# One wide query projection in place of two narrow ones, ahead of an expert layer's row gathers

## The reference

```
def peer(xn, wq, subkeys, u, v):              # xn: 256 x 2048
    q = (xt @ wq).reshape(T, 8, 2, 128)       # wq: 2048 x 2048, 8 heads, 2 sides
    s1 = einsum('thd,nd->thn', q[:, :, 0], subkeys[0])      # 128 keys on each side
    s2 = einsum('thd,nd->thn', q[:, :, 1], subkeys[1])
    v1, i1 = top_k(s1, 16);  v2, i2 = top_k(s2, 16)
    sc, ci = top_k(all 16 x 16 sums of v1 and v2, 16)
    idx = i1[ci // 16] * 128 + i2[ci % 16]    # 128 experts of each token
    gate = softmax(sc)
    h = gelu(xc . u[ic])                      # u: 16384 x 2048, rows gathered by idx
    return sum over the 128 of gate * h * v[ic]             # v: 16384 x 2048
```

## Time and profile before

| | |
|---|---|
| median of 3 runs | 3982.63 us |
| lowest and highest run | 3982.62 and 3986.85 us |
| profiled execution: span from first to last instruction | 3985.6 us |
| profiled execution: own time | not listed apart; its span is 3.0 us over the median and 1.25 us under the highest run |
| TensorE busy | 2187.0 us, 55% of the span |
| VectorE busy | 1962.2 us, 49% |
| GpSimd busy | 1297.3 us, 33% |
| ScalarE busy | 343.6 us, 9% |
| moved by DMA | 932.83 MB, 637.57 MB of it on the queue of GpSimd's gathers and loads |

### The profile page before, as it was taken

The page is one execution under the profiler, slowest core; times in us unless marked ns, Lnnn a source line. Parts: engine busy times, 40 slices in busy tenths (PEclk is TensorE's granted clock), DMA queues, the critical chain, the costliest instruction groups (busy, mean ns, idle before and its releaser), DMA issues.

```text
span 3985.6 us, 26773 instructions
## 1 busy us (share of the span) xinstructions
PE 2187.0 (55%) x8774; PEld 1503.0 (38%) x8774; DVE 1962.2 (49%) x2297; ACT 343.6 (9%) x713; POOL 1297.3 (33%) x712
## 2 busy tenths in 40 slices
PE   0899853588999999998898898700000000000000
PEld 0444642545888887443448756700000000000000
DVE  7664165311000000001004511799998888888887
ACT  0000222101011110000103501000000000000000
POOL 2111140000000000000000000177788888888886
PEclk9999875789999999999997999955555555555555
DMA  9898200023444444443640035799899999999998
GB/s 375 333 416 349 67 34 0 1 86 136 157 148 152 153 148 147 157 148 115 203 144 18 0 110 187 282 403 411 341 416 391 374 390 372 374 373 376 378 359 340
DMA packets 236362, 932.83 MB, mean 234 GB/s; under 512 B 20059, under 2 KB 25363, under 8 KB 164115
## 3 DMA queue, kind: packets, MB, share of 16 engines
q0 software_dynamic: 99840, 637.57, 40.1%
q1 hardware_dynamic: 136197, 294.46, 21.7%
q10 hardware_dynamic: 272, 0.13, 0.0%
HBM read 928.91 MB, written 2.15 MB: 234 GB/s over the span
## 4 chain that ended last, share of the span: by engine, by line
PE 50%; DVE 22%; DMA 10%; POOL 8%; issue 6%; ACT 2%; DVEq 0%; SPq 0%; POOLq 0%; ACTq 0%
PE ps L789 16%; PE ps L1041 15%; PE ps L1054 8%; DVE x L1811 6%; POOL ring L456 4%; DVE ring L1773 4%; DVE proj L1773 4%; PE ps L1189 3%; POOL proj L456 3%; DMA ring<-in_w_in 3%; DMA proj<-in_peer_v,proj 2%; DMA ring<-in_peer_u,proj 2%; DMA ring<-in_peer_v,proj 2%; DMA arena<-in_w_mod 1%; DVE arena L1261 1%
## 5 line engine op out<-in xcount | busy, mean ns | idle before, releaser
L447 POOL COPY proj<-proj 128x8 int32 x64 | 109.8, 1716 | 1999.7 <-DVE proj L1746 1957.0
L1041 PE MATMUL ps<-hT,ring 128*128 128x256 f32 x2816 | 608.0, 379 | 1.4 <-ACT hT L488 1.4
L1041 PEld LDWEIGHTS ps<-hT,ring 128*128 128x128 f32 x2816 | 535.0, 190 | 74.3 <-issue 1.7
L789 PE MATMUL ps<-ring,hT 128*128 128x512 f32 (+2 forms) x1216 | 492.8, 567 | 12.1 <-DMA ring<-in_w_in 10.7
L1811 DVE SCALAR_TENSOR_TENSOR x<-proj,x 128x2048 f32<-128x2048 f32 x128 | 301.3, 2354 | 84.2 <-DMA proj<-in_peer_v,proj 73.7
L789 PEld LDWEIGHTS ps<-ring,hT 128*128 128x128 f32 x1216 | 226.1, 197 | 279.0 <-issue 255.4
L1811 DVE SCALAR_TENSOR_TENSOR x<-ring,proj,x 128x2048 f32<-128x2048 f32 x128 | 301.0, 2352 | 30.2 <-DMA ring<-in_peer_v,proj 13.4
L1054 PE MATMUL ps<-ring,arena 128*128 128x512 f32 x704 | 304.1, 595 | 2.7 <-ACT arena L651 2.7
L456 POOL DMA_INDIRECT ring<-in_peer_v,proj x128 | 291.9, 2281 | 39.0 <-issue 39.0
L1773 DVE CUSTOM_DVE_ANT_0 proj<-proj,yT 128x2048 f32<-128x2048 f32 x128 | 288.5, 2289 | 21.4 <-DMA proj<-in_peer_u,proj 18.2
L1773 DVE CUSTOM_DVE_ANT_0 ring<-ring,yT 128x2048 f32<-128x2048 f32 x128 | 289.5, 2292 | 18.6 <-DMA ring<-in_peer_u,proj 17.5
(11 more groups left out here) (379 smaller groups left out, 2250.8 us busy)
## 6 DMA issues: line engine op xcount, KB each, us to landing
arena<-in_w_mod POOLq DMA_DIRECT2D x96, 1024.0 KB
ring<-in_w_in SPq DMA_DIRECT2D x68, 1024.0 KB, 12.8
ring<-in_ffn_w_gate SPq DMA_DIRECT2D x44, 1024.0 KB, 5.1
ring<-in_ffn_w_up SPq DMA_DIRECT2D x44, 1024.0 KB, 5.2
ring<-in_ffn_w_down SPq DMA_DIRECT2D x44, 1024.0 KB, 4.8
ring<-in_w_out SPq DMA_DIRECT2D x32, 1024.0 KB, 5.1
ring<-in_peer_wq SPq DMA_DIRECT2D x32, 1024.0 KB, 5.0
arena<-bias_rows SPq DMA_DIRECT2D x1, 4096.0 KB, 14.4
```

The costliest lines, as they stand in the source:

```text
L447: pool_eng.tensor_copy(expert_now[:, half, :], expert[:, t, bass.ds(i * (2 * ROWS) + ROWS * half, ROWS)]).then_inc(sem("experts_now"), 1)
L789: ins = pe.matmul(ps[:, 2 * (b % 2) + t, 0:w], lhs[:, KS * s + k, P * t:P * (t + 1)], ring[:, s, k, 0:w], start=(s == 0 and k == 0), stop= ...
L1041: ins = pe.matmul(ps[:, 4 * m + f, 0:T], ring[:, s, k, P * f:P * (f + 1)], hT[:, KS * s + k, :], start=(s == 0 and k == 0), stop=(s == SLO ...
```

## The change

TensorE now runs the query projection once, with both token tiles as 256 moving columns: four blocks in place of eight, in banks 0 to 3 and 4 to 7 in turn. The weights are streamed once. ScalarE copies 4 x 256 columns for each block. The second block waits for `keys_out`, since the turned keys lie in bank 4. After the fourth block's copy come tile 0's scores into banks 0 to 3 and at once tile 1's into banks 4 to 7, and ScalarE copies eight banks out. VectorE's and GpSimd's programs stay as they were, but for the block count in GpSimd's wait and one small memset that is dropped.

```diff
-for _n, _c in (... ("out2", 4), ("wq", 8)):
+for _n, _c in (... ("out2", 4), ("wq", 4)):
...
-        for t in range(NT):
-            stream(w1v["peer_wq_2"], BLK["wq"] + 4 * t, 4, 0)
+        stream(w1v["peer_wq_2"], BLK["wq"], 4, 0)
...
-                                pool_eng.wait_ge(*at("unit_used", SLOTS * (BLK["wq"] + 4 * NT)))
+                                pool_eng.wait_ge(*at("unit_used", SLOTS * (BLK["wq"] + 4)))
...
+        with act.Fori(0, 2) as i:
+            for par in range(2):
+                act.wait_ge(*at("unit_used", i * (2 * SLOTS) + SLOTS * (BLK["wq"] + par + 1)))
+                act.copy(peer["q"][:, bass.ds(i * 8 + 4 * par, 4), :], ps[:, 4 * par:4 * par + 4, 0:T]).then_inc(sem("wq_out"), 1)
         for t in range(NT):
-            with act.Fori(0, 4) as i:
-                act.wait_ge(*at("unit_used", i * SLOTS + SLOTS * (BLK["wq"] + 4 * t + 1)))
-                act.copy(peer["q"][:, bass.ds(i * 4, 4), P * t:P * (t + 1)], ps[:, 0:4, 0:P]).then_inc(sem("wq_out"), 1)
             for b in range(4):
                 act.wait_ge(*at("keys_scored", t * 4 + b + 1))
-                act.copy(peer["score"][:, t, 4 * b:4 * b + 4, :], ps[:, 4 + b, :]...).then_inc(sem("score_out"), 1)
+                act.copy(peer["score"][:, t, 4 * b:4 * b + 4, :], ps[:, 4 * t + b, :]...).then_inc(sem("score_out"), 1)
...
+        def wq_block(i, par):
+            for s in range(SLOTS):
+                pe.wait_ge(sem(f"slot{s}"), i * 32 + 16 * (BLK["wq"] + par + 1))
+                for k in range(KS):
+                    for f in range(4):
+                        ins = pe.matmul(ps[:, 4 * par + f, 0:T], ring[:, s, k, P * f:P * (f + 1)], hT[:, KS * s + k, :],
+                                        start=(s == 0 and k == 0), stop=(s == SLOTS - 1 and k == KS - 1))
+                ins.then_inc(sem("unit_used"), 1)
+
+        wq_block(0, 0)
+        pe.wait_ge(*at("keys_out", 1))
+        wq_block(0, 1)
+        for par in range(2):
+            pe.wait_ge(*at("wq_out", par + 1))
+            wq_block(1, par)
+        pe.wait_ge(*at("wq_out", 4))
         for t in range(NT):
-            with pe.Fori(0, 4) as i:
-                ...
-            pe.wait_ge(*at("wq_out", 4 * t + 5))
-            if t == 0:
-                pe.wait_ge(*at("keys_out", 1))
-            else:
-                pe.wait_ge(*at("score_out", 4))
             for c in range(SIDES):
-                ins = pe.matmul(ps[:, 4 + c // 4, P * (c % 4):P * (c % 4 + 1)], ...)
+                ins = pe.matmul(ps[:, 4 * t + c // 4, P * (c % 4):P * (c % 4 + 1)], ...)
...
-        link(vec.memset(stat[:, 24:25], 0.0), "wq_out")
```

More of the change, by code:

```diff
@@ L54 @@
 _b = 0
-for _n, _c in (("in1", 12), ("out1", 4), ("up", 22), ("down", 11), ("in2", 7), ("out2", 4), ("wq", 8)):
+for _n, _c in (("in1", 12), ("out1", 4), ("up", 22), ("down", 11), ("in2", 7), ("out2", 4), ("wq", 4)):
     BLK[_n] = _b
@@ L723, in _ @@
         norm_cols(3, vc("ffn_norm2", 0, 16), None)
+        with act.Fori(0, 2) as i:
+            for par in range(2):
+                act.wait_ge(*at("unit_used", i * (2 * SLOTS) + SLOTS * (BLK["wq"] + par + 1)))
+                act.copy(peer["q"][:, bass.ds(i * 8 + 4 * par, 4), :], ps[:, 4 * par:4 * par + 4, 0:T]).then_inc(sem("wq_out"), 1)
         for t in range(NT):
-            with act.Fori(0, 4) as i:
-                act.wait_ge(*at("unit_used", i * SLOTS + SLOTS * (BLK["wq"] + 4 * t + 1)))
-                act.copy(peer["q"][:, bass.ds(i * 4, 4), P * t:P * (t + 1)], ps[:, 0:4, 0:P]).then_inc(sem("wq_out"), 1)
             for b in range(4):
                 act.wait_ge(*at("keys_scored", t * 4 + b + 1))
-                act.copy(peer["score"][:, t, 4 * b:4 * b + 4, :], ps[:, 4 + b, :].rearrange("p (a b) -> p a b", b=P)).then_inc(sem("score_out"), 1)
+                act.copy(peer["score"][:, t, 4 * b:4 * b + 4, :], ps[:, 4 * t + b, :].rearrange("p (a b) -> p a b", b=P)).then_inc(sem("score_out"), 1)
         for t in range(NT):
@@ L1180, in _ @@
         ins.then_inc(sem("keys_turned"), 1)
-        for t in range(NT):
-            with pe.Fori(0, 4) as i:
[L1184 to L1191, removed]
-            pe.wait_ge(*at("wq_out", 4 * t + 5))
-            if t == 0:
-                pe.wait_ge(*at("keys_out", 1))
-            else:
-                pe.wait_ge(*at("score_out", 4))
+        def wq_block(i, par):
[13 more added lines that the diff above has]
+        pe.wait_ge(*at("wq_out", 4))
+        for t in range(NT):
             for c in range(SIDES):
-                ins = pe.matmul(ps[:, 4 + c // 4, P * (c % 4):P * (c % 4 + 1)], peer["q"][:, c, P * t:P * (t + 1)], peer["keysT"][:, c % 2, :],
+                ins = pe.matmul(ps[:, 4 * t + c // 4, P * (c % 4):P * (c % 4 + 1)], peer["q"][:, c, P * t:P * (t + 1)], peer["keysT"][:, c % 2, :],
                                 start=True, stop=True)
```

## The result

The changed kernel takes 4031.43 us (median of 4 runs, 4029.68 to 4038.03) against 3983.47 us (4 runs, 3982.62 to 3986.85): ratio 1.0121, interval 1.0107 to 1.0136, or +48.0 us. The forecast was 4029 us in a range of 4020 to 4038, +46.8 us.

What follows compares the result with a forecast made beforehand. The start of the second stage, through tile 0's scores and choice, bounds the kernel; a delay is carried to the end. Terms +50.3 - 7.9 + 4.4 = +46.8 us, giving 4029 us on the median, range 4020 to 4038.

Steps and rivals of the forecast that it cites:

- The hinge: Query projection between the two stages: it matters by when the second stage can begin, not by how busy TensorE is.
- Projection, +50.3 us: Joint pass of 512 instructions with 256 columns takes 110.5 us, so tile 0's scores start 50.3 us later.
- Rival B: Projection pass: weight loading sets the pitch at 0.192 us, pass 98.3 us, 12 us less, 4017 us; chance 2%.
- Weights, `keys_out`, the memset, straight code: 0 each: Around the projection: saved weight traffic, the wait for turned keys, the dropped memset and unlooped TensorE code each change nothing.
- Choice, 52.7 us: VectorE's choice of tile 0's experts: same instructions, still 52.7 us, experts at 2608.4.
- ScalarE's wait, -7.9 us: Before tile 0's dot products: the 13.96 us wait falls to 2.6; they begin 7.75 us after the experts, not 15.7.
- Arrival of the slots, +4.4 us: First sixteen dot products: gathered slots arrive at DMA's pace, not already waiting, losing 3.6 to 5.4 us.
- -3.5: Lead left at the first dot products after slower slot arrival: 2.5 to 4.3 us, taken as 3.5.
- "The shift stays.": After the first dot products: group pitch 41.07 us is VectorE's, DMA needs 39.4 to 41.2, so the delay persists.
- Rival C: Gather stages from 2922 us on settle into another beat, 10 us either way: 4019 or 4040; chance 5%.
- the prediction's chances: Whole kernel: slower 98%, 1% faster 1%, the same 1%; the forecast itself 91%.

Runs made afterwards that it cites:

- wait_both: The kernel before, with VectorE beginning tile 0's choice only when both tiles' scores are out (score_out 8 in place of 4); ratio 1.0145.
- pick_later: The kernel before, with tile 0's pick_weights and its wait for ScalarE's exponential moved behind the first sixteen dot products; ratio 0.9998.
- wide_early: The changed kernel, with both tiles' four sides of each block scored and chosen while the next block runs; ratio 1.0091 to the kernel before.
- the three early kernels: Choice cut by blocks: on the kernel before 1.0048, the same with each slot's gather freed by own last use 1.0035, on the changed kernel 1.0091.

## Why the prediction was right, step by step

**The hinge.** The prediction read that the choice for tile 0, not TensorE's second pass, feeds the next stage, although the chain named the pass. wait_both shows it: a start of the choice 65 us later, and nothing else, costs 58 us.

**Projection, +50.3 us.** Measured +50.5 (the pass 110.7 us, predicted 110.5; the copy 1.01). The price from the row of the same shape held to 0.2 us. Rival B falls by the same row. By the spacings of the Trainium skill, "TensorE: Matmul & The Clock Gate", section "Back-to-back issue gap", the pass would have taken an estimated 94 us; this trace disagrees, 0.216 us an instruction.

**Weights, `keys_out`, the memset, straight code: 0 each.** TensorE has no gap between its 512 matmuls, with idle time 0.0 in its group.

**Choice, 52.7 us.** Measured 52.7.

**ScalarE's wait, -7.9 us.** Measured -8.4: the first dot product 7.3 us after the experts, predicted 7.75. The term was right in size and in what is late next (the first slot), usable 5.6 us after its gather was issued where the prediction added up 6.06. The exponential was cheaper than the 2.6 us taken: its table load ran 48.77 us ahead of its activation, in ScalarE's idle time.

**Arrival of the slots, +4.4 us.** The first group is 5.0 us longer, the whole stage 3.6 and 6.0. With the term before it this makes -4.8 and -2.4 in place of -3.5. pick_later, which has these two terms almost alone, ends at 0.9998, so their sum cannot be told from nothing.

**"The shift stays."** Right, but one reason was wrong in part. The prediction took the first stage's pitch as VectorE's because VectorE was 99% busy. wide_early shows that the rate of the gathers stays the same with VectorE relieved; GpSimd, which the prediction called nearly full only from 2922 us on, may hold it as well as the DMA engines. Had the change moved tile 1's choice out of the dot products, the prediction would have credited a gain that isn't there; my own expectations for the three early kernels made that mistake.

**Rival C and the scatter.** The stages from the first dot product to the end did scatter, 1402 to 1418 us over the kernels that keep their order of work, the changed and the unchanged alike. The forecast of the time was within 2.4 us of the median, in part by luck: that scatter is larger than the miss. The v additions take 716 to 721 us in nine profiles and 725 to 730 in three; in these three GpSimd's own instructions take 605 to 610 us of the stage, in the others 595 to 600. Why they do stays open. In the prediction's chances those that make the kernel slower add up to 99%, not 98%; nothing hangs on it.

## What to carry to other kernels

Merging two passes for fewer instructions and half the bytes delays the first result to the end of the joint pass; where the next stage starts from the first result, that delay is the price, and no saving in the merged stage pays it back if that stage's end was not the limit. When two paths end close together the chain shows only the later one: find when the other was ready. And before work is moved off an engine that looks full, see whether a second resource (here the DMA engines and GpSimd) is full beside it, or start its stream earlier instead; that was the one thing here that gained.

## What the hardware showed that was not expected

- The table load of an activation can run far ahead of it: in the changed kernel 1.28 us at 2568.85, the exponential at 2618.91, behind a 48.77 us wait. In the kernel before, ScalarE came to the load only at 2571.17, behind the copies of tile 1's scores, and VectorE had to wait for it.
- The same attention code took 180.6 us in one execution and 189.3 to 193.5 us in the eleven others. TensorE's mean granted clock over the stage was 0.95 in the one and 0.86 to 0.89 in the others.
- Two 128-column matmuls in a row with the same weights cost 0.1118 us each, against 0.1138 with new weights each time.
- GpSimd takes 0.94 us to issue a gather of 128 rows while VectorE is idle or searches maxima, and 1.9 to 3.1 us for most of those beside dot products or v additions (2.06 and 2.24 us on average in the kernel before).
